# Raw weight copies landed where their low parts go, and expert blocks loaded from the dense layer on

## The reference

```
for layer in (0, 1):
    u = rmsnorm(x) @ w_mix_in[layer]                  # 1024 x 3088
    mixed = concat(dilated_attention, gated_linear_attention, short_conv)   # from parts of u
    x = x + mixed @ w_mix_out[layer]                  # 1024 x 1024
    h = rmsnorm(x)
    if layer == 0:
        f = (silu(h @ ffn_w1) * (h @ ffn_w3)) @ ffn_w2          # hidden width 2816
    else:
        f = sum_e gate[e] * ((silu(h @ w1[e]) * (h @ w3[e])) @ w2[e])   # top 2 of 8, width 3584
    x = x + f
out = rmsnorm(x)
```

## Time and profile before

| | |
|---|---|
| time, median of 3 runs | 1298.56 us (1297.44 to 1298.94) |
| profiled execution | 1295.39 us, of which the span of its instructions is 1293.6 us |
| TensorE matmul busy | 1251.1 us, 97% of the span |
| DVE, ACT busy | 382.4 us (30%), 246.3 us (19%) |
| mixer 0, dense layer, mixer 1, experts | from about 0, 133, 323 and 450 us |
| transfers | 430.74 MB, 333 GB/s over the span |

### The profile page before, as it was taken

The page is one execution under the profiler, slowest core; times in us unless marked ns, Lnnn a source line. Parts: engine busy times, 40 slices in busy tenths (PEclk is TensorE's granted clock), DMA queues, the critical chain, the costliest instruction groups (busy, mean ns, idle before and its releaser), DMA issues.

```text
span 1293.6 us, 29466 instructions
## 1 busy us (share of the span) xinstructions
PE 1251.1 (97%) x13303; PEld 732.9 (57%) x13303; DVE 382.4 (30%) x484; ACT 246.3 (19%) x328; POOL 23.0 (2%) x38
## 2 busy tenths in 40 slices
PE   9999999999999999999999999999799999999775
PEld 6998888888999833453433643453243453355222
DVE  4777644444667520111120111002012002011102
ACT  5654543333573300000000000000000000000001
POOL 3000000000100000000000000000000000000000
PEclk9999999999999999999999999999999999999998
DMA  9842745523746899999999999999999999999994
GB/s 312 297 158 98 265 176 174 182 97 116 277 168 235 348 413 404 407 365 414 411 411 412 414 409 413 413 411 411 415 411 412 411 408 406 412 414 397 409 411 202
DMA packets 115972, 430.74 MB, mean 333 GB/s; under 512 B 10615, under 2 KB 17047, under 8 KB 101378
## 3 DMA queue, kind: packets, MB, share of 16 engines
q1 hardware_dynamic: 114226, 423.48, 83.5%
q0 software_dynamic: 1616, 5.33, 1.2%
HBM read 427.72 MB, written 2.11 MB: 332 GB/s over the span
## 4 chain that ended last, share of the span: by engine, by line
PE 87%; DMA 11%; DVE 1%; ACT 1%; issue 0%; SPq 0%; POOL 0%; POOLq 0%; DVEq 0%
PE psum L1907 34%; PE psum L1927 17%; PE psum L1428 9%; PE psum L1430 9%; PE psum L1429 9%; DMA ring<-in_moe_w 9%; PE psum L1644 1%; DMA ring<-in_moe_w_end 1%; PE psum L1881 1%; PE psum L1964 1%; PE psum L1856 1%; PE psum L1447 1%; PE psum L1780 0%; PE psum L1603 0%; PE psum L1604 0%; DMA x<-in_x 0%
## 5 line engine op out<-in xcount | busy, mean ns | idle before, releaser
L1907 PE MATMUL psum<-ring,xe 128*32 128x512 f32 (+1 forms) x5376 | 518.8, 541 | 18.5 <-DMA ring<-in_moe_w 13.5
L1907 PEld LDWEIGHTS psum<-ring,xe 128*32 128x32 f32 x5376 | 168.9, 110 | 348.1 <-issue 271.0
L1927 PE MATMUL psum<-ring,gT 128*32 128x256 f32 x4640 | 259.0, 379 | 9.0 <-DMA ring<-in_moe_w 9.0
L1927 PEld LDWEIGHTS psum<-ring,gT 128*32 128x32 f32 x4640 | 148.1, 110 | 123.3 <-issue 17.2
L1287 DVE TENSOR_TENSOR gate<-gate,psum 128x768 f32<-128x768 f32 (+3 forms) x32 | 24.5, 767 | 511.0 <-ACT gate L831 511.0
L926 DVE TENSOR_TENSOR wlo<-raw,whi 128x2048 fp32r<-128x2048 f32 (+1 forms) x66 | 145.3, 2228 | 58.7 <-ACT whi L657 58.7
L831 ACT ACTIVATE gate<-psum 128x768 f32<-128x768 f32 (+3 forms) x32 | 21.2, 661 | 611.0 <-PE psum L1907 611.0
L657 ACT CAST whi<-raw 128x2048 fp32r<-128x2048 f32 (+1 forms) x66 | 120.2, 1861 | 56.8 <-PE psum L1430 32.5
L1428 PE MATMUL psum<-whi,f_hi 128*128 128x512 f32 (+1 forms) x320 | 123.8, 387 | 1.0 <-DVE wlo L926 0.9
L1430 PE MATMUL psum<-whi,f_lo 128*128 128x512 f32 (+1 forms) x320 | 121.4, 379 | 0.0
L1429 PE MATMUL psum<-wlo,f_hi 128*128 128x512 f32 (+1 forms) x320 | 121.3, 379 | 0.0
(11 more groups left out here) (249 smaller groups left out, 774.1 us busy)
## 6 DMA issues: line engine op xcount, KB each, us to landing
ring<-in_moe_w SPq DMA_DIRECT2D x384, 512.0 KB, 14.9
ring<-in_moe_w SPq DMA_DIRECT2D x112, 1024.0 KB, 18.3
raw<-in_ffn_w SPq DMA_DIRECT2D x33, 1024.0 KB, 5.7
ring<-in_moe_w_end SPq DMA_DIRECT2D x64, 512.0 KB, 16.8
raw<-in_w_mix_in SPq DMA_DIRECT2D x21, 1024.0 KB, 7.4
raw<-in_w_mix_out SPq DMA_DIRECT2D x8, 1024.0 KB, 5.5
raw<-in_w_mix_in SPq DMA_DIRECT2D x4, 544.0 KB, 6.1
x<-in_x SPq DMA_DIRECT2D x2, 512.0 KB, 4.2
```

The source lines that it names most:

```text
L1907: ins = mm(banks(j, n)[o:o + 32, g, 0:2 * q].rearrange("p (i b c) -> p i b c", i=2, c=128), rows_[:, k * CAP + 32 * g:k * CAP + 32 * (g + 1)],
L1927: ins = mm(bank[bk][32 * q:32 * (q + 1), at_:at_ + 256], gT[j % 2][:, a:a + 32], w[:, o:o + 256], start=j == 0 and n == 0 and at_ == 0, st ...
```

## The change

The three fixed raw buffers and the three in the mixers' area are gone. A block's raw copy is loaded into the buffer of its `wlo`, and DVE subtracts in place. There are six raw buffers everywhere, one for each slot, and a load now waits for `block_used` of the block that had the slot before; the split waits for the load alone. Blocks 51 on take the slots in another order (`slot_of`), since PE is done with the last dense blocks in another order (`used_after`). The space of the three fixed raw buffers takes expert blocks 1, 2 and 3. These and block 0 are asked for one at a time by `early`: after the dense chunks 0, 1 and 3, and after block 50's load. On ACT and DVE, `split(b + 15)` and `split(b + 16)` move down between later levels, and the second w2 split of a dense chunk moves behind `d_gT`.

```diff
+def slot_of(n):
+    if n <= BASE[1]:
+        return n % SLOTS
+    return (BASE[1] + (3, 4, 1, 2, 5, 0)[(n - BASE[1] - 1) % SLOTS]) % SLOTS
+def used_after(n):
+    late = {BASE[1] - 5: 2, BASE[1] - 4: 2, BASE[1] - 3: -2, BASE[1] - 2: -2}
+    return n + 1 + late.get(n, 0)
...
-        raw_at = at[0]
-        raw = [place(f"raw{i}", BLOCK) for i in range(RAW_FIXED)]
+        early_at = at[0]
+        at[0] += 4 * BLOCK * EARLY_FIXED
...
+        raw = [place(f"raw{i}", BLOCK, offset=w_at[1] + 4 * BLOCK * i) for i in range(SLOTS)]
...
-                until = None if before is None else sp.lower_val(per * turn + before + 1)
+                until = None if free is None else sp.lower_val(per * turn + free)
...
-                    load.wait_op(lo_ready, until, "sem-ge")
+                    load.wait_op(block_used, until, "sem-ge")
...
+                    if l and i == 0:
+                        early(EARLY - 1)
...
-                        if c == 0 and i == 1 and k == 1:
-                            sp.wait_ge(mix_ready, 4)
...
+            def early(b):
+                load_up(0, 0, 0, 0, range(b, b + 1))
...
             dense_chunk(0, 0)
+            early(0)
             dense_chunk(1, 0)
+            early(1)
             with sp.Fori(0, DENSE_FULL - 3) as c:
                 dense_chunk(2, c)
+            early(2)
             dense_chunk(DENSE_FULL - 1, 0)
...
-                    for k in range(2):
-                        split(n + 4 + k, turn, 6)
+                    split(n + 4, turn, 6)
                     d_gT(c, 0, turn)
+                    split(n + 5, turn, 6)
```

More of the change, by code:

```diff
@@ L84 @@
 SLOTS = 6
-RAW_FIXED = 3
+EARLY_FIXED = 3
 K_ID, K_IOTA, K_DOWN = 0, P, 2 * P
@@ L99, in block_size, with uses_of, slot_free @@
     return BLOCK
[L102 to L111, removed]
+def slot_of(n):
+    if n <= BASE[1]:
+        return n % SLOTS
+    return (BASE[1] + (3, 4, 1, 2, 5, 0)[(n - BASE[1] - 1) % SLOTS]) % SLOTS
+def uses_of(n):
+    return sum(slot_of(i) == slot_of(n) for i in range(n + 1))
+def used_after(n):
+    late = {BASE[1] - 5: 2, BASE[1] - 4: 2, BASE[1] - 3: -2, BASE[1] - 2: -2}
+    return n + 1 + late.get(n, 0)
+def slot_free(n):
+    before = [i for i in range(n) if slot_of(i) == slot_of(n)]
+    return used_after(before[-1]) if before else None
 def shape_constants():
@@ L226, in trunk @@
         setup_router = place("setup_router", 64, offset=base["bias0"] + 5 * 2048 + 256)
-        at[0] = ffn_arena
-        raw += [place(f"raw{i}", BLOCK) for i in range(RAW_FIXED, SLOTS)]
+        at[0] = ffn_arena + 3 * 4 * BLOCK
         gate_out = [place(f"gate_out{i}", FC) for i in range(2)]
@@ L254, in trunk @@
         assert max(mix_end, dense_end) <= spare_at
-        pairs_at = [w_at[i] + 8192 * ((MOE0 - SLOTS + n) % SLOTS) for n in range(SLOTS) for i in range(2)]
-        ring_at = [spare_at] + [raw_at + 8192 * i for i in range(RAW_FIXED)]
+        pairs_at = [w_at[i] + 8192 * slot_of(MOE0 - SLOTS + n) for n in range(SLOTS) for i in range(2)]
+        ring_at = [spare_at] + [early_at + 8192 * i for i in range(EARLY_FIXED)]
         ring_at += pairs_at[0:6] + [ffn_arena + 8192 * i for i in range(ARENA)] + pairs_at[6:]
@@ L478, in free_slot @@
                 slot = ring_slot(f)
[L479 to L481 removed]
+                if EARLY <= f < EARLY + 6:
                     sp.wait_ge(block_used, MOE0 - SLOTS + 1 + (f - EARLY) // 2)
@@ L533, in chosen_expert @@
                 return sp.value_load(order[0:1, ds(at_, 1)], min_val=0, max_val=EXPERTS - 1)
+            def early(b):
+                load_up(0, 0, 0, 0, range(b, b + 1))
             def sweep_experts(sweep):
-                load_up(PER_SWEEP * sweep, 0, 0, 0)
+                load_up(PER_SWEEP * sweep, 0, 0, 0, range(0 if sweep else EARLY, KD))
                 expert(sweep, 0, 0)
@@ L649, in split @@
             def split(n, turn=0, per=0):
-                s, w = raw_slot[n], n % SLOTS
+                w = slot_of(n)
                 size = block_size(n)
[L653 to L657, removed]
+                act.wait_ge(raw_full[w], 16 * (per // SLOTS) * turn + 16 * uses_of(n))
+                nc.scalar.copy(whi[w][:, 0:size], raw[w][:, 0:size]).then_inc(hi_ready, 1)
             def norm_squares(i, t):
@@ L745, in mixer @@
                     nc.scalar.copy(pT[:, 512 * j:512 * (j + 1)], bank[j][:]).then_inc(pT_sb, 1)
-                split(b + 15)
-                split(b + 16)
                 level_decay(2)
                 level_decay(3)
+                split(b + 15)
                 level_decay(4)
                 level_decay(5)
+                split(b + 16)
                 level_decay(6)
@@ L1373, in _ @@
                 norm_row(0, t)
-            first = raw[raw_slot[0]]
+            first = raw[0]
             dve.wait_ge(hi_first, 1)
@@ L1803, in dense_up @@
                 if c < DENSE_FULL:
-                    blocks = [((n + k) % SLOTS, 4, 6 * turn + n + k + 1) for k in range(2)]
+                    blocks = [(slot_of(n + k), 4, 6 * turn + n + k + 1) for k in range(2)]
                     width = FC
@@ L1807, in dense_up @@
                     n = DENSE0 + 6 * c + i
-                    blocks = [(n % SLOTS, 8, n + 1)]
+                    blocks = [(slot_of(n), 8, n + 1)]
                     width = HALF
@@ L1817, in dense_down @@
                 if c < DENSE_FULL:
-                    blocks = [((n + k) % SLOTS, 6 * turn + n + k + 1) for k in range(2)]
+                    blocks = [(slot_of(n + k), 6 * turn + n + k + 1) for k in range(2)]
                 else:
                     n = DENSE0 + 6 * c + 2
-                    blocks = [(n % SLOTS, n + 1)]
+                    blocks = [(slot_of(n), n + 1)]
                 down(4 + 2 * t, gT_hi[t], gT_lo[t], blocks, c == 0, c == DENSE_FULL, gT_ready,
```

25 lines of the change are left out of this document (11 added, 14 removed).

## The result

The changed kernel takes 1308.88 us (median of 4 runs, 1307.08 to 1310.18) against 1298.0 (4 runs, 1297.29 to 1298.94): ratio 1.0082, 95% interval 1.0065 to 1.01. It is slower, by close to what was predicted (1309). The profiled execution took 1307.68 us, span 1305.9, granted clock 0.993; before it was 1295.39, 1293.6 and 0.996. The span grew by 12.3 us.

The account below looks back on a forecast made before the run. TensorE's own work was taken to bound the kernel up to about 450 us; in the expert stage, transfers end the waits. 0 + 7.2 + 0.6 + 2.8 = 10.6 us slower than the 1298.56 median gave 1309, range 1303 to 1314.

Parts of the forecast that it names:

- Early blocks, 0: Expert stage: the four expert blocks loaded early gain 0, bounds 0 and 10.2 us.
- the full ring: Expert loads: ring buffers full by 460 us either way, state at 550 us the same, so earlier loading gains 0.
- The rival of bytes by rate: Expert stage: length is bytes by rate, 4 MB loaded beforehand save 10.2 us, time 1299.0; chance 0.08.
- The splits moved down, 3.6 in each mixer: Mixers' last levels: two splits on DVE delay level 8 and first projection; TensorE loses 3.6 us each, 7.2 together.
- 4.5 less 0.78 of pauses used up: DVE up to the conv product: two splits' time less pauses of 0.49 and 0.29 us, moving it from 413.61 to 417.3.
- The wait for f_lo: First projection in each mixer: TensorE waits about 1 us for DVE's low part, after about 2.5 us at level 8.
- Split 19, 0.6: End of mixer 0: split ahead of the residual add on DVE makes the norm's transposes 0.6 us late (0 to 1.0).
- Dense turns, 2.8: Gate turns behind dense chunks 1 and 3: an expert load delays block loads, 1.4 us each, 2.8 together, bounds 0 and 4.4.
- the rival that the chunks are covered: Dense chunks: the loads catch up, so the 2.8 us is not lost and the time is 1306.4; chance 0.15.
- The clock: Both mixers: the clock falls as TensorE stands 2.5 us, does level 8 and stands about 1 us more; chance 0.17.
- The shift ahead of the experts: Expert stage only shifts, delay passing in full: first expert block at 464 to 465 instead of 453.97, ring waits 27 to 29 us.
- Moved splits free: Mixers: the moved splits cost nothing, only 3.4 us left at most, time 1299 to 1302; chance 0.05.

Follow-up runs that it names:

- the second: The changed kernel run again without any further change, in the first group of experiments: 1309.39 us, ratio 1.0101 against the kernel before.

## Why the prediction was right, by its own steps

**Early blocks, 0.** Right. The stage behind the gather had its waits for the ring and its gap in the DMA engines at the places that the full ring predicts. Its length goes with the clock at its head and not with the early blocks, over all profiles:

| half clock at the head | expert stage with early blocks | without |
|---|---|---|
| none | | 830.7 |
| 3.4 us | 831.1 | 832.1 (before), 832.1 |
| 6.8 | | 833.5 |
| 10.2 | 834.2, 835.0, 835.1, 833.9 | 835.0, 834.8 |
| 13.7 | 835.2, 835.3 | |

The rival of bytes by rate wanted 822 us in the column with early blocks. It falls.

**The splits moved down, 3.6 in each mixer.** Right in place, mechanism and the wait named (2.3 us for scores at level 8, 2.5 predicted); oversized as a term, 3.1 measured in mixer 0 and 3.1 in both once the clock was kept up. The failing piece is "4.5 less 0.78 of pauses used up". From one start to the next the rows say it: the two splits push what is behind them by 2.20 us each (410.42 to 412.62, 418.82 to 421.02), 4.40 and not 4.49 (the first split's printed end is 410.42 + 2.28 = 412.70, and the next instruction starts at 412.62). And from `level_operands(5)` to the conv product before was 404.27 to 413.61, 9.34 us; now 410.42 to 422.86, 12.44 with the first split in it. 4.40 less 3.10 is 1.30 us absorbed: the two pauses that I counted, one of 0.21 us inside the stretch that I had left out, and a rest of 0.3, whose cause no run shows. The wait for f_lo was predicted as a further 1 us. In the first profile it is 0.41 us in mixer 0, where the clock stayed up, and in mixer 1 level 8 at half clock hides it. So of the shift of 3.1 us, 2.3 are the wait for the scores and 0.4 that for f_lo.

**Split 19, 0.6.** Right in place; 0.8 measured as a shift, 0.6 as a wait. The load landed after 5.0 us, as taken. Putting the split lower gave 0.9 back.

**Dense turns, 2.8.** Right: 3.1 in the first profile, 2.5 in the second and 2.1 to 2.2 in the three other kernels that kept these loads, at the two chunks named. The cover without an expert block was 0.84 us for my 0.8. The loads behind `ring1` landed 8.5, 8.5, 8.0 and 7.9 us after their issue in the first profile, where the turn lost 2.0 us, and 7.7, 7.7, 7.2 and 7.1 in the second, where it lost 1.2; in chunk 2, which no expert block disturbs, it was 4.8 to 5.2. So the rival that the chunks are covered falls. It comes nearly true if the blocks are asked for behind chunk 0; even then 0.9 remain.

**The clock.** I gave it 0.17 as a rival and left it out of the sum. It belongs in it. In each of the 6 profiles with the pause of 2.3 us in mixer 1 the clock was 0.50 for 3.4 us or more behind it; in mixer 0 it was in 4 of 7; where the pause was absent or filled with spare matmuls, in no mixer 1 (7 profiles). The upper end of my range has room for 1.7 us a stretch, my estimate from half of the 3.42 us at 0.50 in the earlier trace rows. No run shows that price; measured is 1.0 to 1.6 us for 3.4 us at half clock (16.6 to 17.2 us against 15.7) and 2.4 us for 6.8 (18.1). I did not follow where the rest of 0.1 to 0.7 goes. That the time came out at 1309 in spite of the clock is partly luck. By terms, the profiled execution had the levels 1.0 below my sum, the norm and the turns 0.5 above, the start 0.9 below, half clock in mixer 1 1.1 above and the longer half clock at the experts' head 2.1 above: 1.8 in all, where 1307.68 less 1306.0 is 1.7.

Whether the experts' longer half clock comes from the change is not shown, and the record speaks against it. Kernels without the pause in mixer 1 had none, 3.4, 6.8 and 10.2 us there, those with it 3.4, 10.2 and 13.7. Of the 57 executions of the kernel before that ran beside the experiments, 21 had a granted clock of 0.995 or 0.996 over the span and took 1295.0 to 1296.1 us, and 36 had 0.990 to 0.994 and took 1296.2 to 1299.7. The one profiled for the earlier trace rows is of the first kind, with 0.996. As an estimate, 0.003 less clock over 1294 us is 7.8 us more at half clock, about the 6.8 by which 10.2 exceeds 3.4. So the kernel before probably had the long half clock in most of its executions, and the 2.1 us at the experts' head probably come from which execution was profiled, not from the change. None of those 36 was profiled, so this stays an inference. It would also account for most of the 3.2 us that I added from profile to median. In medians the change cost 10.9 us (1308.88 less 1298.0), for the 10.6 of the sum.

**The shift ahead of the experts.** Right: the gather starts at 460.16 instead of 449.87, 10.3 us later. The first expert block, at 466.58, is 12.7 us later and not the 10 to 11 that I named, since the gather in between ran at a clock of 0.50 (from 460.8 us). The waits for the ring, 26.5 us, are just under the 27 to 29 named and far from the 20 that would have spoken for bytes by rate.

**Moved splits free.** Falls: with nothing else changed they bring a ratio of 1.0071.

## What to carry to other kernels

Where an engine works without pause, ask of each instruction that is moved onto its list what stands behind it, and who waits for that; the same two splits left the step at 12.6 us in one place and brought it to 15.7 in another, a few levels further down. Measure the room that is left from start to start over the whole stretch, not from printed durations and the idle times one happens to see. And a full ring buffer erases what was loaded early (here 4 MB ahead of the experts left their stage at 831.1 us, against 832.1 without, where bytes by rate promised 10.2): look at whether the loader waits for the consumer before counting bytes.

## What the runs showed of the hardware

A pause of 2.3 us in TensorE's work was followed by 3.4 us at a granted clock of 0.50 (once 6.8) in 6 of 6 cases in mixer 1 and 4 of 7 in mixer 0, and 1.9 us of wait was followed by it once in two. Waits of 1.8 us had none behind them: one at a gate's turn (206.0 us in the changed kernel's first profile) and one in the expert stage (1212.6 us in the kernel with mixer 1's splits behind its last level). At the head of the experts there was no half clock, or it lasted 3.4, 6.8, 10.2 or 13.7 us. The twelve profiles whose gather is the same code had 3.4 to 13.7. Four wide matmuls in the gather went with none in the one execution profiled, and only 4 of 12 executions had a span clock that high. What decides between these lengths stays open.
